# Eight PSUM banks in one pool with their own shares in the last sparse branch, a rotation that reads the projection's bank, and residual rows loaded in quarters

## What is computed

```python
h = _rmsnorm(x, g_in); proj = h @ w_in        # split into a_*, b_*, c_*, gates
y_a = sliding window attention with sinks (a_q, a_k rotated), 8 heads, 2 kv heads
y_b = for each query the top 256 keys by an indexer's score
      (b_qi, b_ki rotated), attention over them, 8 heads, one kv head
y_c = 4-head attention into rmsnorm(mem) @ w_mem_kv
ys = stack([y_a * silu(a_z), y_b * silu(b_z), y_c * silu(c_z)])
u = einsum('bsnc,ncd->bsnd', ys, w_branch)
merged = sum(sigmoid(gates) * u, over the three)
out = _rmsnorm(x + merged @ w_out, g_final)

def _rope(x, cos, sin):
    x1, x2 = jnp.split(x, 2, axis=-1)
    return jnp.concatenate([x1 * cos - x2 * sin, x2 * cos + x1 * sin], axis=-1)
```

## Time and profile before

| | us |
|---|---|
| median of 3 runs | 2916.28 (2912.83 to 2922.0) |
| the profiled execution | 2915.3 |
| its span, first to last instruction | 2913.5 |
| mean granted clock of TensorE | 0.956 |

### The profile page before, as it was taken

One profiled execution on the slowest core, in us unless ns is written; L12 is line 12 of the kernel. 1 busy time (PEld: TensorE's weight loads), 2 busy tenths in 40 slices (PEclk: granted clock), 3 DMA queues, 4 the chain that ended last, 5 costly groups with the idle time before them and its releaser, 6 DMA issues.

```text
span 2913.5 us, 37353 instructions
## 1 busy us (share of the span) xinstructions
PE 2564.3 (88%) x13093; PEld 2122.5 (73%) x13093; DVE 1795.1 (62%) x3558; ACT 1362.4 (47%) x2760; POOL 536.6 (18%) x488
## 2 busy tenths in 40 slices
PE   5898999988889989998888989998888888878996
PEld 4676878766778878876667778887666777667785
DVE  6457666224667677216778788721688887677521
ACT  4454644333646444215646445521566672444511
POOL 4435354442020200101020110010101002000010
PEclk8899999999999999999999999999999899999998
DMA  5556575784443522564243421155424234000154
GB/s 168 190 170 206 171 245 174 240 257 146 151 152 123 167 73 66 195 203 151 97 150 109 146 79 52 44 202 195 144 87 139 100 99 133 29 30 30 37 184 148
DMA packets 172346, 399.36 MB, mean 137 GB/s; under 512 B 13568, under 2 KB 96512, under 8 KB 162176
## 3 DMA queue, kind: packets, MB, share of 16 engines
q1 hardware_dynamic: 172160, 396.96, 41.3%
HBM read 308.31 MB, written 88.60 MB: 136 GB/s over the span
## 4 chain that ended last, share of the span: by engine, by line
PE 40%; DVE 20%; ACT 15%; issue 14%; POOL 6%; DMA 3%; SPq 1%; DVEq 0%; ACTq 0%; POOLq 0%
PE bank L858 28%; ACT signs L1023 4%; PE PV L825 4%; PE TR L757 4%; ACT prob L988 3%; ACT prob L998 3%; DVE ptL L1394 2%; ACT ptH L1012 2%; POOL fL L1174 2%; DVE nmx L1363 2%; DVE prob L1353 2%; DVE score L1615 2%; POOL turn L1250 1%; PE bank L768 1%; DVE zs L1425 1%
## 5 line engine op out<-in xcount | busy, mean ns | idle before, releaser
L858 PE MATMUL bank<-hH,pairs 128*128 128x512 f32 (+1 forms) x3584 | 1166.0, 396 | 21.1 <-DVE zs L1457 7.8
L858 PEld LDWEIGHTS bank<-hH,pairs 128*128 128x128 f32 x3584 | 683.9, 193 | 162.3 <-issue 23.1
L858 PE MATMUL bank<-hL,pairs 128*128 128x512 f32 (+2 forms) x1792 | 707.6, 395 | 0.0
L1023 ACT ACTIVATE signs<-score,bits 128x384 int8<-128x384 f32 (+7 forms) x256 | 335.8, 1312 | 274.1 <-DVE bits L1495 261.0
L1394 DVE TENSOR_TENSOR ptL<-TR,ptH 128x512 fp32r<-128x512 f32 (+1 forms) x384 | 256.8, 670 | 263.5 <-ACT ptH L1012 260.3
L858 PEld LDWEIGHTS bank<-hL,pairs 128*128 128x128 f32 (+1 forms) x1792 | 346.0, 193 | 66.4
L1012 ACT ACTIVATE ptH<-TR 128x512 fp32r<-128x512 f32 (+1 forms) x384 | 219.5, 575 | 336.8 <-PE TR L757 335.9
L1476 DVE TENSOR_SCALAR_CACHE_REDUCE above<-score,bits 128x256 uint8<-128x256 f32 (+10 forms) x280 | 348.1, 1243 | 9.5
L757 PE MATMUL TR<-identR,prob 128*128 128x128 f32 x1480 | 235.2, 281 | 99.6 <-ACT prob L998 52.2
L757 PEld LDWEIGHTS TR<-identR,prob 128*128 128x128 f32 x1480 | 180.0, 143 | 176.2 <-ACT prob L998 65.7
L1164 POOL TENSOR_TENSOR pairs<-raw,pairs 128x512 fp32r<-128x512 f32 x164 | 217.8, 1338 | 327.8 <-ACT pairs L957 327.6
(11 more groups left out here) (206 smaller groups left out, 3880.1 us busy)
## 6 DMA issues: line engine op xcount, KB each, us to landing
pairs<-w_split SPq DMA_DIRECT2D x444, 512.0 KB, 3.5
w_split<-pairs SPq DMA_DIRECT2D x74, 1024.0 KB, 5.0
raw<-in_w_in SPq DMA_DIRECT2D x106, 256.0 KB, 5.6
xs<-in_x SPq DMA_DIRECT2D x4, 2048.0 KB, 9.2
rows<-in_x SPq DMA_DIRECT2D x4, 2048.0 KB, 9.2
out<-rows SPq DMA_DIRECT2D x4, 2048.0 KB, 7.5
table<-trig SPq DMA_DIRECT2D x48, 128.0 KB, 3.2
raw<-in_w_branch SPq DMA_DIRECT2D x24, 256.0 KB, 5.6
```

Of the source, the lines that this page charges most:

```text
L858: done = nc.tensor.matmul(PJ[st.u + half * up][0:min(st.width, P), 0:st.n_tok], lhs, rhs[:, row, 0:st.n_tok], start=(n % 12 == 0 and (up o ...
L1023: nc.scalar.activation(signs[:, 0:keys], score[:, tt, 0:keys], ACT.Sign, bias=thr.bitcast(F32)[:, tt:tt + 1], scale=-1.0, accum_out=cnt[:, ...
```

## The change

- `take_bank` now serves all eight banks in four kinds: pj, s, pv and tr. Outside the last group's sparse branch the shares are as before. In that branch (`three_for_scores(True, g == NG - 1)`) one bank serves projections, two scores, two value products and three what is turned; before it was 2, 3, 1 and 2.
- The rotation: VectorE multiplies the projection's bank by sin into fT and by cos into turn; ScalarE rounds fT to fH; GpSimd takes fL; TensorE swaps; VectorE adds the bank to turn. GpSimd's product and sum go, in all groups. For kv and kiw ScalarE still copies the upper half of the bank.
- The rows are loaded a quarter at a time, one after each of the output units 1 to 4, with the final gain behind the last.

```diff
+    last_use, turn_of = [None] * 8, dict(pj=0, s=0, pv=0, tr=0)
+    kinds = dict(pj=(0, 1, 2), s=(3, 4), pv=(5,), tr=(6, 7))
...
+    def three_for_scores(yes, long=False):
         kinds["pj"], kinds["s"] = ((0, 1), (2, 3, 4)) if yes else ((0, 1, 2), (3, 4))
+        kinds["pv"], kinds["tr"] = (5,), (6, 7)
+        if long:
+            kinds["pj"], kinds["s"], kinds["pv"], kinds["tr"] = (0,), (3, 4), (5, 2), (6, 7, 1)
...
-            st.evac = event("act_pj")[1]
-            if role in ("z", "mk", "cq"):
+            if role not in ROPED or role in ("kv", "kiw"):
+                st.evac = event("act_pj")[1]
+            if role in ("z", "mk", "cq") + ROPED:
                 pj_freed.append(event("dve_pj"))
...
-                    f_freed.append(("roped", st.k + 1))
+                    f_freed.append(("tr_full", swaps[-1] + 1))
...
-        three_for_scores(True)
+        three_for_scores(True, g == NG - 1)
         attention("b", g, branch_units(0, g, 2, 12), 24, 0)
...
-        steps.append(Step("load_rows", g=g, x=count["pool_x"]))
...
         for m in range(KC):
             last_out = unit("out", "w_out", m * P, moving="m", m=m, g=g, y=n["y"])
+            if 1 <= m <= NT:
+                steps.append(Step("load_rows", g=g, tt=m - 1, x=count["pool_x"]))
...
                     sp.wait_ge(S["pool_x"], st.x)
-                    sp.dma_start(rows[:, :, :], x_v[st.g]).then_inc(S["rows_in"], 16)
-                    sp.dma_start(gfin[:, :], g_final.unsqueeze(0).broadcast_to([P, D])).then_inc(S["gfin_in"], 16)
+                    sp.dma_start(rows[:, st.tt, :], x_v[st.g, :, st.tt, :]).then_inc(S["rows_in"], 16)
+                    if st.tt == NT - 1:
+                        sp.dma_start(gfin[:, :], g_final.unsqueeze(0).broadcast_to([P, D])).then_inc(S["gfin_in"], 16)
...
-                if tr >= 2:
-                    pe.wait_ge(S["tr_free"], tr - 1)
+                wait_bank(banks_of["tr"], tr)
...
-                if j == 0 and it.pv:
-                    pe.wait_ge(S["dve_pv"], it.pv)
+                if j == 0:
+                    wait_bank(banks_of["pv"], it.pv)
...
-                if st.role in ROPED + ("av", "mv"):
+                if st.role in ("av", "mv"):
                     wait_free(act, f_freed, st.f)
                     nc.scalar.activation(staged(st)[0:st.width, 0:st.n_tok], bank, ACT.Copy).then_inc(S["act_pj"], 1)
+                elif st.role in ROPED:
+                    lanes = rows_of(st)
+                    if st.role in ("kv", "kiw"):
+                        wait_free(act, f_freed, st.f)
+                        nc.scalar.activation(staged(st)[HD:st.width, :], PJ[st.u][HD:st.width, :], ACT.Copy).then_inc(S["act_pj"], 1)
+                    act.wait_ge(S["f_sin"], st.k + 1)
+                    if st.k:
+                        act.wait_ge(S["tr_full"], swaps[st.k - 1] + 1)
+                    nc.scalar.activation(fH[lanes, :], staged(st)[lanes, :], ACT.Copy).then_inc(S["f_hi"], 1)
...
-                    if st.g:
-                        if st.k >= 4:
-                            pool.wait_ge(S["stack_lo"], st.k - 3)
-                        nc.gpsimd.tensor_tensor(turn[lanes, st.k % 4, :], f[lanes, :], table[lanes, 0, :], ALU.mult).then_inc(S["f_cos"], 1)
...
-                elif st.kind == "rope":
-                    lanes = rows_of(st.unit)
-                    pool.wait_ge(S["tr_free"], st.tr + 1)
-                    pool.wait_ge(S["f_cos"], st.k + 1)
-                    nc.gpsimd.tensor_tensor(turn[lanes, st.k % 4, :], turn[lanes, st.k % 4, :], staged(st.unit)[lanes, :],
-                                            ALU.add).then_inc(S["roped"], 1)
...
-                dve.wait_ge(S["f_cos"], st.k + 1)
-                TT(staged(st.unit)[lanes, :], TR[st.tr % 2][lanes, :], table[lanes, 1, :], ALU.mult).then_inc(S["tr_free"], 1)
+                dve.wait_ge(S["dve_pj"], st.unit.used)
+                TT(turn[lanes, st.k % 4, :], TR[st.tr][lanes, :], turn[lanes, st.k % 4, :], ALU.add).then_inc(S["tr_free"], 1)
...
-                    dve.wait_ge(S["act_pj"], st.evac)
-                    if st.k:
-                        dve.wait_ge(S["tr_full"], swaps[st.k - 1] + 1)
-                    nc.vector.tensor_copy(fH[lanes, :], staged(st)[lanes, :]).then_inc(S["f_hi"], 1)
-                    if not st.g:
-                        if st.k >= 4:
-                            dve.wait_ge(S["stack_lo"], st.k - 3)
-                        TT(turn[lanes, st.k % 4, :], staged(st)[lanes, :], table[lanes, 0, :], ALU.mult).then_inc(S["f_cos"], 1)
+                    if st.role in ("kv", "kiw"):
+                        dve.wait_ge(S["act_pj"], st.evac)
+                    dve.wait_ge(S["tile_done"], st.wt + 1)
+                    wait_free(dve, f_freed, st.f)
+                    TT(staged(st)[lanes, :], PJ[st.u][lanes, :], table[lanes, 1, :], ALU.mult).then_inc(S["f_sin"], 1)
+                    if st.k >= 4:
+                        dve.wait_ge(S["stack_lo"], st.k - 3)
+                    TT(turn[lanes, st.k % 4, :], PJ[st.u][lanes, :], table[lanes, 0, :], ALU.mult).then_inc(S["dve_pj"], 1)
```

More of the change, by code:

```diff
@@ L91, in take, with take_turned @@
         return n[name] - k
+    def take_turned(k=1):
+        for _ in range(k):
+            take_bank("tr", ("tr_free", take("tr") + 1))
+        return n["tr"] - k
     def event(name):
@@ L153, in turned @@
                 if st.role in ("av", "mv", "kv", "kiw"):
-                    steps.append(Step("turn", unit=st, tr=take("tr")))
+                    steps.append(Step("turn", unit=st, tr=take_turned()))
                     f_freed.append(("tr_full", n["tr"]))
                 if st.role in ROPED:
-                    swaps.append(take("tr"))
+                    swaps.append(take_turned())
                     steps.append(Step("rope", unit=st, k=st.k, tr=swaps[-1], first=(st is units[0])))
@@ L171, in turned @@
                 if st.role in ROPED:
-                    steps.append(Step("halve", unit=st, k=st.k))
+                    steps.append(Step("halve", unit=st, k=st.k, tr=swaps[-1]))
         if finishing is not None:
@@ L192, in finish @@
         for half in range(first, last):
-            steps.append(Step("finish", g=g, tr=take("tr"), i=half, evac=last_out.evac))
+            steps.append(Step("finish", g=g, tr=take_turned(), i=half, evac=last_out.evac))
     def finish_rows(g):
@@ L201, in norm @@
         for k in range(first, last):
-            steps.append(Step("norm", source=source, g=g, i=n["normed"], k=k, tr=take("tr")))
+            steps.append(Step("norm", source=source, g=g, i=n["normed"], k=k, tr=take_turned()))
         if last == KC:
@@ L256, in attention @@
             it.groups = -(-it.keys // (2 * P)) if branch == "b" else 2
-            it.tr, it.p = take("tr", it.groups), take("p", it.groups)
+            it.tr, it.p = take_turned(it.groups), take("p", it.groups)
             group.items.append(it)
@@ L301, in order_of_work @@
     norm("mem", 0)
-    steps.append(Step("inverse", tr=take("tr")))
+    steps.append(Step("inverse", tr=take_turned()))
     prepare("x", 0)
```

66 lines of the change are left out of this document (32 added, 34 removed).

## The result

| | before | after |
|---|---|---|
| median | 2917.19 us (2912.83 to 2922.0, 4 runs) | 2829.92 us (2821.06 to 2832.68, 4 runs) |
| ratio | | 0.9695, 95% interval 0.9669 to 0.9722 |
| profiled execution, span | 2913.5 us | 2827.4 us |
| mean granted clock of TensorE | 0.956 | 0.968 |

The forecast was 2860 us, a gain of 56; the kernel gained 87. The time lies at the very edge of the range (2830 to 2892), outside by 0.1 us, which is far less than its own runs differ by; what the experiments show to be wrong are the sizes of two of the three terms, in opposite directions.

What follows compares the result with a forecast made beforehand. TensorE's queue, busy 88% of the span, was taken to bound the kernel. From 2915.3 us, rows -30, rotation -28 and banks +2 gave 2859.3, with 1.0 to the median 2860 us; range 2830 to 2892.

Steps and rivals of the forecast that it cites:

- part 2: Rotation units in all stages: taking GpSimd's product and sum away gains 28 us, bounds 12 to 40.
- Part 1, the rows: Output stages: loading residual rows in quarters ends waits for weights, gaining 30 us, 9 of them in the first group.
- Part 2, the loop: Windowed preparation, groups 1 to 3: threshold out at about t+3.2, 1.1 us gained a turn, 13 us in all.
- The race that the rival feared: Rotation gives nothing (0.10, 2888 us), one form: fL starting behind a selection step ends 0.8 us later, 19 us lost.
- Part 2, group 0: First group's windowed preparation loop: GpSimd's freed room is filled by splitting weights, so no gain was taken.
- Part 2, the other preparations: Windowed and sparse attention starts gain 8 us; preparations of the sparse branch, keys and index gain 7 us.
- Part 3, the banks: Last group's sparse branch: new bank shares gain and cost nearly alike, net 2 us slower, bounds -50 to +60.
- the gains that it counted as 17: Last sparse branch: second value bank and third transpose bank save 17 us of TensorE's waits, and 2 of clock.
- The cost of the single projection bank: Last sparse branch: 13 handovers of the one projection bank, 28.5 us late, of which 15 us kept as cost.
- the term for the clock: Last sparse branch: slow granted clock after the longer new waits costs 2.5 us.
- The banks cost what the lateness says: Rival, chance 0.12: the last sparse branch's banks cost +45 us, so 2903 us.
- The two signs named for a wrong forecast: Last sparse branch moving by over 15 us either way, or the windowed preparation's loop not shortening.

Runs made afterwards that it cites:

- free reading passes: The whole change with GpSimd's two passes per rotated unit put back as products reading a constant tile, nobody waiting for them: 2857.67 us, ratio 0.9805.
- only a write in the chain: The whole change with GpSimd's passes back as constant writes, the addition, ScalarE's halves and VectorE's low halves waiting for them: 2854.62 us, ratio 0.9793.
- a read in it: The whole change with GpSimd's passes back as products reading two tables, the whole rotation chain waiting for them: 2913.96 us, ratio 0.9995.
- the old shares: The whole change, but the last group's sparse branch keeps 2 projection, 3 score, 1 value and 2 turned banks: 2812.17 us, ratio 0.9652.

## Why the prediction was right or wrong

The miss is in part 2: its sum of 28 us measured 66. By the parts alone the forecast of 2860 becomes 2837: 38 us less for the rotation, 13 more for the banks, 2 more for the rows. The last 7 us are what the parts give together beyond their sum, within what the intervals leave open. That the total came so near the range is luck in part: the banks' miss hid a third of the rotation's.

**Part 1, the rows, right.** Forecast -30, alone -28 us (34 in the output stages themselves, in both kernels). ScalarE's copies in the output stage of group 1, as in the earlier trace rows:

```profile
1206.58 0.60 ACT L1069 ACTIVATE ob<-bank 128x512 f32<-128x512 f32 x1 [4.58 <-PE bank L871]
1212.49 0.60 ACT L1069 ACTIVATE ob<-bank 128x512 f32<-128x512 f32 x1 [4.74 <-PE bank L871]
1218.43 0.60 ACT L1069 ACTIVATE ob<-bank 128x512 f32<-128x512 f32 x1 [4.75 <-PE bank L871]
```

5.91 and 5.94 us apart where one gap was 12.22. The stage's DMA engines move 234 GB/s at a clock of 1.00; the four stages shrank by 10.8, 6.3, 9.7 and 7.5 us, where the forecast had 9 for the first and 21.4 for the others. The quarters held up no weights, in group 0 neither.

**Part 2, the loop, right in its mechanism and to a tenth.** One turn in the last group's windowed preparation:

```profile
2161.03 0.69 DVE L1451 TENSOR_TENSOR fT<-bank,table 128x512 f32<-128x512 f32 x1
2161.64 0.68 DVE L1454 TENSOR_TENSOR turn<-bank,table 128x512 f32<-128x512 f32 x1
2162.24 0.68 DVE L1341 TENSOR_TENSOR turn<-TR,turn 128x512 f32<-128x512 f32 x1
2162.84 0.91 DVE L1495 TENSOR_TENSOR bits<-small 128x4 int32<-128x4 f32 x1
2163.78 0.17 DVE L1499 SCALAR_TENSOR_TENSOR bits<-bits 128x4 int32<-128x4 int32 x1
2163.98 0.17 DVE L1507 TENSOR_SCALAR bits<-bits 128x4 int32<-128x4 int32 x1
2164.19 1.95 DVE L1488 TENSOR_SCALAR_CACHE_REDUCE above<-score,bits 128x1664 uint8<-128x1664 f32 x1
```

The three full steps run at t, t+0.6 and t+1.2 (t = 2161.03), the first integer step is held to 0.91 us by fL, the other two take 0.17 as in the earlier trace rows, the threshold is out at t+3.16 (forecast 3.2), and the next turn begins at 2174.14, 9.95 us later (forecast about 10, before 11.08). GpSimd in those turns:

```profile
2162.47 1.26 POOL L1196 TENSOR_TENSOR fL<-fT,fH 128x512 fp32r<-128x512 f32 x1 [8.69 <-ACT fH L1056]
2172.42 1.26 POOL L1196 TENSOR_TENSOR fL<-fT,fH 128x512 fp32r<-128x512 f32 x1 [8.69 <-ACT fH L1056]
```

The 13 us for the loops of groups 1 to 3 are 14.5 in the kernel with the rotation alone. The race that the rival feared was not lost: over all units fL takes 1.28 us in the mean where it took 1.37 before.

**Part 2, group 0, the step that failed.** "In group 0 GpSimd also splits weights, which fill the room; I take nothing there." That was said of the loop; for the keys and index units of all groups stood "7 us over all". Group 0 gave 24.3 us, 12.2 of them ahead of its index scores. The reasoning looked at what a free GpSimd would fill its time with, not at what stood behind its queue. Before, in order of time, at the index queries of group 0:

```profile
108.54 1.27 POOL L1164 TENSOR_TENSOR pairs<-raw,pairs 128x512 fp32r<-128x512 f32 x1
109.77 1.27 POOL L1250 TENSOR_TENSOR turn<-turn,fT 128x512 f32<-128x512 f32 x1
```

```profile
111.08 2.55 ACT L1098 ACTIVATE qst<-turn 64x512 fp32r<-64x512 f32 x4 [6.84 <-POOL turn L1250]
```

```profile
102.61 3.78 DVE L1601 TENSOR_TENSOR qst<-turn,qst 64x512 fp32r<-64x512 f32 x4 [5.67 <-ACT qst L1098]
...
107.37 0.68 DVE L1329 TENSOR_TENSOR fT<-TR,table 128x512 f32<-128x512 f32 x1
...
113.66 3.78 DVE L1601 TENSOR_TENSOR qst<-turn,qst 64x512 fp32r<-64x512 f32 x4 [5.62 <-ACT qst L1098]
```

VectorE's product is done at 108.05. The sum starts 1.7 us later, behind a weight half, and ends at 111.04. ScalarE stands 6.84 us; the last 3.0 of them are that queue and the sum. One unit takes 11.05 us. After, with the sum on VectorE:

```profile
97.95 3.79 DVE L1613 TENSOR_TENSOR qst<-turn,qst 64x512 fp32r<-64x512 f32 x4 [2.63 <-ACT qst L1120]
...
102.98 0.67 DVE L1341 TENSOR_TENSOR turn<-TR,turn 128x512 f32<-128x512 f32 x1
...
106.27 3.79 DVE L1613 TENSOR_TENSOR qst<-turn,qst 64x512 fp32r<-64x512 f32 x4 [2.62 <-ACT qst L1120]
```

8.32 us a unit, and the 5.07 us that TensorE stood before, for the keys of the index, are gone:

```profile
121.65 0.77 PE L858 MATMUL bank<-hH,pairs 128*128 128x512 f32 x1 [5.07 <-DVE kiS L1601]
```

That it is the place in the chain and not the reading is shown by the kernels above: up to the index scores of group 0 the change takes 118.5 us, 119.6 with free reading passes, 125.2 with only a write in the chain and 129.4 with a read in it, as long as before (129.3).

**Part 2, the other preparations, too small.** 8 us for the attention starts and 7 for the rest stood for what measured 27.9 us in groups 1 to 3 alone (7.8, 7.2 and 12.9 by stages). The sum was counted as one step of 1.3 us at each start and priced from TensorE's wait at L889, whose 50.7 us gave the upper bound of 40. It was no bound: 18.4 of them went. The price stood in other rows of the same list, those of the steps between (us, times, longest), before:

```profile
ACT qst L1098 <- POOL turn L1250: 146.2, 28, 9.5
...
DVE qst L1601 <- ACT qst L1098: 84.5, 35, 5.7
```

and after:

```profile
DVE qst L1613 <- ACT qst L1120: 41.4, 28, 2.6
ACT qst L1120 <- DVE turn L1341: 32.5, 23, 6.0
```

ScalarE's halves stood 146.2 us for GpSimd's sum and stand 32.5 for VectorE's. And only in the loop was VectorE priced as held by GpSimd. That was right for the larger part: of the 20.6 us between the profiled executions of the change and of the free reading passes, 11 are in the four windowed preparations. Five to 6 are in the preparations of the sparse branch, for which the forecast had no such term.

**Part 3, the banks, right in what would be seen and wrong in its price.** Forecast +2, alone +15, and between the change and the old shares 12 by the ratios and 18 by the medians. Of the earlier trace rows, ptL is 0.6 us and zs has no row: the gains that it counted as 17 are made and given back at the scores, 22.5 us. The cost of the single projection bank was taken as 15 us of waits and measured 21.5 (nine of thirteen handovers had one, and 28.5 was the sum of the list), 2.0 more stand right behind the branch, and the term for the clock, 2.5 us, was the worst: 10 us in the branch. It was priced for all waits together, while five of the nine new ones, of 2.59 to 4.38 us, have half-level matmuls behind them, as the rows above show.

**The rivals.** None came in. "The banks cost what the lateness says" had the right mechanism for part 3; together with the real gain of part 2 it is hidden in a total that looks better than the forecast. The two signs named for a wrong forecast, the branch moving by over 15 us and the loop not shortening, did not show either: the branch moved by 9 and the loop did as told. They watched the two places that had been worked out and not the one that had been left at nothing.

## What to carry to other kernels

When work leaves an engine, go through its queue at every stage and ask who stood behind it there, also where that engine stays busy: in group 0, where GpSimd has weights to split as well, its leaving brought 24 us against 14 in each other group. Take reading passes off GpSimd first where VectorE works from SBUF beside it; passes that only write cost 3 us here even at three times the number. In this branch the projections, whose banks are read late, needed two; the banks that TensorE fills ahead of VectorE could be shared out in several ways within 5 us, since the wait mostly moved.

## What the runs showed of the hardware

GpSimd's passes beside VectorE: 91 reading passes over 52 units that nobody waits for cost 28 us; with writes of 1.6 us in their place 3 us. VectorE was busy for 29.8 us more in the one case and 5.1 in the other. Its step of 4 integers in a row took 301 ns in the mean beside these reading passes, 324 beside those that read two tiles, and 221 beside the writes; a step with an input in PSUM did not change (682 and 681 ns).

The granted clock: each of five waits of TensorE at one bank, of 2.59 to 4.38 us, was followed by a matmul of 0.77 us at a clock of 0.50, where 0.47 at 1.00 follows a wait of 0.7 us. Nine waits at that bank, 21.5 us, went with a mean of 0.92 in place of 0.95 over some 300 us and 10 us more of matmul time, about half of their own length; the waits that stood in the branch with the old shares, 21.1 and 16.2 us in 30 pieces, had left the mean at 0.95.
